# Thirty-two modulation rows of a fused transformer kernel moved from GpSimd to VectorE chains beside the first expert tables

## The reference, cut to what matters

```python
for l in range(DEPTH):                      # first block, DEPTH = 2
    mod = silu(c) @ mod_w[l] + mod_b[l]
    sh1, sc1, g1, sh2, sc2, g2 = split(mod, 6)
    h = rmsnorm(x) * (1 + sc1) + sh1
    y = gla_mixer(h) if l == 0 else swa_sink_attention(h, k_sh, v_sh)
    x = x + g1 * y
    h = rmsnorm(x) * (1 + sc2) + sh2
    x = x + g2 * peer(h)                    # u = u_tab[e], gelu(h . u), times gate, times v_tab[e]
    # behind layer 0: shared keys and values, with a modulation of their own
# second block: one layer, retention + latent attention with (sh1, sc1, g1), experts with (sh2, sc2, g2)
```

## Time and profile before

| | |
|---|---|
| median of 3 runs | 3168.49 us (3166.95 to 3172.3) |
| the profiled execution: its own time | 3162.82 us |
| its span | 3161.0 us |
| mean granted clock of TensorE | 0.972 |
| PE / DVE / ACT / POOL busy | 2972.8 / 2045.1 / 1586.9 / 1596.7 us |
| bytes read from memory | 550.17 MB |

### The profile page before, as it was taken

One profiled execution on the slowest core, in us unless ns is written; L12 is line 12 of the kernel. 1 busy time (PEld: TensorE's weight loads), 2 busy tenths in 40 slices (PEclk: granted clock), 3 DMA queues, 4 the chain that ended last, 5 costly groups with the idle time before them and its releaser, 6 DMA issues.

```text
span 3161.0 us, 57822 instructions
## 1 busy us (share of the span) xinstructions
PE 2972.8 (94%) x18908; PEld 2689.0 (85%) x18908; DVE 2045.1 (65%) x3383; ACT 1586.9 (50%) x3103; POOL 1596.7 (51%) x1261
## 2 busy tenths in 40 slices
PE   7989999988999986999999799999899999999998
PEld 6779999987787875899999677887789789999997
DVE  6648960058888878389200888887883446777776
ACT  1124555577555543355555965554454224555554
POOL 5868898986544445159989844443470010000100
PEclk8989999999999997999999999999999999999998
DMA  7545555522766632345555056664464235555553
GB/s 249 206 155 182 184 180 182 183 73 94 258 233 228 230 137 87 128 155 185 179 181 190 7 186 244 231 234 175 176 224 134 93 127 193 192 192 195 192 192 125
DMA packets 153462, 552.56 MB, mean 175 GB/s; under 512 B 16896, under 2 KB 19712, under 8 KB 153232
## 3 DMA queue, kind: packets, MB, share of 16 engines
q1 hardware_dynamic: 151136, 547.42, 49.9%
q10 hardware_dynamic: 2224, 3.87, 0.4%
HBM read 550.17 MB, written 1.05 MB: 174 GB/s over the span
## 4 chain that ended last, share of the span: by engine, by line
PE 75%; ACT 7%; DVE 6%; issue 5%; POOL 5%; DMA 1%; ACTq 0%; DVEq 0%; SPq 0%; POOLq 0%
PE bank L953 23%; PE bank L979 21%; PE bank L1224 12%; PE bank L1245 6%; PE bank L749 5%; ACT hT L1453 3%; PE bank L697 3%; POOL arena L2562 2%; POOL arena L2564 1%; ACT hT L1449 1%; DVE w_parts L1775 1%; POOL arena L2566 1%; DMA arena<-stream 1%; ACT h_parts L1461 1%; POOL arena L2574 1%
## 5 line engine op out<-in xcount | busy, mean ns | idle before, releaser
L2514 POOL TENSOR_TENSOR w_parts<-ring,w_parts 128x512 fp32r<-128x512 f32 x512 | 665.4, 1308 | 160.6 <-ACT w_parts L1413 113.2
L953 PE MATMUL bank<-h_parts,w_parts 128*128 128x256 f32 x6144 | 738.2, 284 | 3.9 <-POOL w_parts L2514 3.9
L953 PEld LDWEIGHTS bank<-h_parts,w_parts 128*128 128x128 f32 x6144 | 737.5, 192 | 4.3 <-POOL w_parts L2514 4.3
L2562 POOL TENSOR_TENSOR arena<-arena,cact 128x1024 f32<-128x1024 f32 x80 | 165.6, 2070 | 733.5 <-DMA arena<-stream 733.4
L1413 ACT ACTIVATE w_parts<-ring 128x512 fp32r<-128x512 f32 x512 | 323.1, 632 | 319.8 <-PE bank L953 307.6
L1224 PEld LDWEIGHTS bank<-h_parts,w_parts 128*128 128x128 f32 x3072 | 374.8, 193 | 3.9 <-DVE arena L2376 1.5
L1224 PE MATMUL bank<-h_parts,w_parts 128*128 128x256 f32 x3072 | 375.8, 284 | 1.4 <-DVE arena L2376 1.4
L1611 ACT ACTIVATE w_parts<-ring 128x512 fp32r<-128x512 f32 x384 | 242.3, 632 | 266.3 <-PE bank L1224 172.2
L979 PE MATMUL bank<-w_parts,a_parts 128*128 128x512 f32 x1536 | 370.2, 397 | 1.6 <-DVE a_parts L2156 1.6
L979 PE MATMUL bank<-h_parts,a_parts 128*128 128x512 f32 x1536 | 364.5, 393 | 5.6 <-DVE a_parts L2156 5.5
L2445 DVE TENSOR_TENSOR w_parts<-ring,w_parts 128x512 fp32r<-128x512 f32 x376 | 272.4, 736 | 147.7 <-ACT w_parts L1611 144.6
(11 more groups left out here) (339 smaller groups left out, 4628.8 us busy)
## 6 DMA issues: line engine op xcount, KB each, us to landing
ring<-stream SPq DMA_DIRECT2D x786, 512.0 KB, 3.3
arena<-stream SPq DMA_DIRECT2D x192, 512.0 KB, 4.3
hT<-stream SPq DMA_DIRECT2D x32, 512.0 KB, 4.7
mean<-stream SPq DMA_DIRECT2D x32, 512.0 KB, 4.6
arena<-consts ACTq DMA_DIRECT2D x1, 1536.0 KB, 6.6
xT<-xin ACTq DMA_DIRECT2D x1, 1024.0 KB, 10.7
out<-hT SPq DMA_DIRECT2D x4, 256.0 KB, 2.2
arena<-subk ACTq DMA_DIRECT2D x2, 128.0 KB, 2.2
```

The costliest lines, as they stand in the source:

```text
L953: mm = pe.matmul(bank[k][:, 0:T], w[:, wp, ws], h_parts[:, hp, 4 * j + q, :], start=(j == 0 and q == 0 and i == 0), stop=(j == 1 and q == ...
L2514: pool.tensor_tensor(w[:, 1, :], ring[(base + k) % RING][:, j * 512:(j + 1) * 512], w[:, 0, :].bitcast(F32), ALU.subtract).then_inc(sem(f" ...
L2562: pool.tensor_tensor(b3, b3, c_b, ALU.mult).then_inc(sem("mod_step"), 1)
```

## The change

Rows 88 to 103 are now made beside the last 32 tiles of the first table of layer 0, rows 136 to 151 beside those of layer 1 (`UP_FROM` = 96, `UP_ROWS` = 16). SP loads each row into one half of `hT` (two buffers), in `up_loads`, two rows for every four tiles. DVE makes a row in eight dependent steps of 128 x 128 (`up_mods_dve`): one scaled copy from SBUF to PSUM, six times "chunk times scalar plus sum" in PSUM bank 6, and a last one whose output goes to a part in `rs`. The two rows of a turn alternate. PE does the column product behind every second tile, into bank 7, and at the end DVE adds the bias to 16 columns at once. From the attention stage and the mixer the row loads, the POOL work, the column products and the bias additions are gone.

```diff
-MODS_SWA = (88, 104)
-MODS_MIX = (136, 152)
+MODS_UP = ((88, 104), (136, 152))
+UP_ROWS = 16
+UP_FROM = NK - 2 * UP_ROWS
...
+        def up_buffer(i):
+            return hT[:, 4 * i:4 * i + 4, :].rearrange("p c t -> p (c t)")
+        def up_part(i):
+            return rs[:, i * P:(i + 1) * P]
+        def up_loads(sp, l):
+            u, row = MO[f"peer{l}_u"][0], mod_row(MODS_UP[l][0])
+            at = u + UP_FROM
+            def slots(it, lo, hi):
+                for k in range(lo, hi):
+                    s = (at + k) % RING
+                    sp.wait_ge(ring_free, it * RING + (at + k + 1))
+                    sp.dma_start(ring[s][:, :], stream[it * RING + (main_row(at) + k)]).then_inc(landed[s], 16)
+            for i in range(2):
+                sp.wait_ge(ring_free, at)
+                sp.dma_start(up_buffer(i), stream[row + 3 * i]).then_inc(up_landed[i], 16)
+            with sp.Fori(0, UP_ROWS // 2 - 1) as it:
+                for i in range(2):
+                    slots(it, 2 * i, 2 * i + 2)
+                    sp.wait_ge(sem("up_made"), it * 2 + (UP_ROWS * l + i + 1))
+                    sp.dma_start(up_buffer(i), stream[it * 6 + (row + 3 * (i + 2))]).then_inc(up_landed[i], 16)
+            slots(UP_ROWS // 2 - 1, 0, RING)
...
-            loads(MO["peer0_u"][0], after_v[0])
+            loads(MO["peer0_u"][0], MO["peer0_u"][0] + UP_FROM)
+            up_loads(sp, 0)
...
-            loads_with_mods(kv, MO["peer1_q"][0], MODS_SWA, MODS_SWA[0], at)
-            loads(MO["peer1_q"][0], after_v[1])
+            loads(kv, MO["peer1_q"][0])
+            loads(MO["peer1_q"][0], MO["peer1_u"][0] + UP_FROM)
+            up_loads(sp, 1)
...
-            loads_with_mods(mix, MO["mix_out"][1], MODS_MIX, MODS_MIX[0], [mix + 5 * i // 2 for i in range(16)])
+            loads(mix, MO["mix_out"][1])
...
-            up_pe(pe, l, ROUTE_TILE, NK)
+            up_pe(pe, l, ROUTE_TILE, UP_FROM)
+            if l == 0:
+                pe.sem_inc(sem("up_column"), 2)
+            up_pe(pe, l, UP_FROM, NK, rows=True)
...
+                    if rows and k % 2:
+                        i = k // 2
+                        pe.wait_ge(sem("up_made"), it * 2 + (UP_ROWS * l + i + 1))
+                        column(pe, bank[7][:, bass.ds(it * 2 + i, 1)], up_part(i)).then_inc(sem("up_column"), 1)
...
-            project_norm(pe, "swa_out", A.o, "w_out", "1b", between={5: lambda: [mods_pe(pe, MODS_SWA, g) for g in (11, 12)]})
+            project_norm(pe, "swa_out", A.o, "w_out", "1b")
...
-            mods_pe(pe, MODS_MIX, 17)
...
-            mods_pe(pe, MODS_MIX, 18)
...
+        def up_mods_dve(dve, l):
+            lo, hi = MODS_UP[l]
+            sums = [bank[6][:, i * P:(i + 1) * P] for i in range(2)]
+            c = cact[:, 8 * l:8 * l + 8]
+            steps = 2 * (DC - 1)
+            with dve.Fori(0, UP_ROWS // 2) as it:
+                for k in range(DC):
+                    for i in range(2):
+                        w = up_buffer(i)[:, k * P:(k + 1) * P]
+                        if k == 0:
+                            dve.wait_ge(up_landed[i], it * 16 + 16 * (UP_ROWS // 2 * l + 1))
+                            dve.tensor_scalar(sums[i], w, c[:, 0:1], None, ALU.mult).then_inc(sem("up_step"), 1)
+                            continue
+                        dve.wait_ge(sem("up_step"), it * steps + (UP_ROWS // 2 * steps * l + 2 * k - 1 + i))
+                        if k < DC - 1:
+                            dve.scalar_tensor_tensor(sums[i], w, c[:, k:k + 1], sums[i], ALU.mult, ALU.add)\
+                               .then_inc(sem("up_step"), 1)
+                        else:
+                            dve.wait_ge(sem("up_column"), it * 2 + (UP_ROWS * l + i + 1))
+                            dve.scalar_tensor_tensor(up_part(i), w, c[:, k:k + 1], sums[i], ALU.mult, ALU.add)\
+                               .then_inc(sem("up_made"), 1)
+            dve.wait_ge(sem("up_column"), UP_ROWS * (l + 1) + 2)
+            dve.tensor_tensor(modv[:, lo:hi], bank[7][:, 0:hi - lo], V("mod_b")[:, lo:hi], ALU.add).then_inc(signal("dve_step"), 1)
+            dve.wait_ge(sem("dve_step"), signalled("dve_step"))
...
             dve.tensor_scalar(mean[:, 3, :], route[:, 2, :], -1.0, None, ALU.mult).then_inc(sem(f"{n}_negated"), 1)
+            up_mods_dve(dve, l)
             dve.wait_ge(sem(f"{n}_gelu"), NK)
...
-            for g in (11, 12):
-                mods_dve(dve, g)
...
-            behind[("mla_cq", 2)] = lambda: mods_dve(dve, 17)
...
-            mods_dve(dve, 18)
...
-            mods_pool(pool, MODS_SWA, 0)
             peer_pool(pool, 1)
-            mods_pool(pool, MODS_MIX, 1)
```

More of the change, by code:

```diff
@@ L300, in block_program @@
         ring_free = sem("ring_free")
+        up_landed = [sem(f"up_landed{i}") for i in range(2)]
         full = [sem(f"bank_full{i}") for i in range(4)]
@@ L473, in mod_row, with main_row @@
             return SO[f"peer{l}_v"][0] + 3 * (m - (40, 104)[l]) + 2
+        def main_row(i):
+            return i + (40 - FIRST_MODS if i >= FIRST_MODS else 0) + sum(V_ROWS for at in after_v if i >= at)
         def mod_buffers(seg):
@@ L509, in mod_number @@
         def mod_number(m):
-            return m - FIRST_MODS
+            return m - FIRST_MODS - sum(hi - lo for lo, hi in MODS_UP if m >= hi)
+        def up_buffer(i):
[19 more added lines that the diff above has]
+            slots(UP_ROWS // 2 - 1, 0, RING)
         @block.sync
         def _(sp):
-            def main_row(i):
-                return i + (40 - FIRST_MODS if i >= FIRST_MODS else 0) + sum(V_ROWS for at in after_v if i >= at)
             def load(i):
@@ L781, in mods_pe @@
             parts = mod_parts(seg)
[L782 removed]
+            pe.wait_ge(sem("mod_made"), mod_number(8 * g + 7) + 1)
             t = open_tile(f"mods{g}")
@@ L938, in peer_pe, with up_pe @@
             back_pe(pe, n, "kv" if l == 0 else "mid", {0: ((act_y, 1), (dve_y, 1)), 2: ((act_y, 2), (dve_y, 2))})
-        def up_pe(pe, l, first, last):
+        def up_pe(pe, l, first, last, rows=False):
             n = f"p{l}"
-            with pe.Fori(first // 4, last // 4) as it:
+            with pe.Fori(0, (last - first) // 4) as it:
                 for k in range(4):
@@ L946, in up_pe @@
                         half = 2 * k + j
-                        pe.wait_ge(sem(f"{n}_low"), it * 8 + (half + 1))
+                        pe.wait_ge(sem(f"{n}_low"), it * 8 + (2 * first + half + 1))
                         w = w_parts[half % HALVES]
```

12 lines of the change are left out of this document (removed).

## The result

The changed kernel takes **3140.74 us** (median of four runs, 3138.13 to 3149.34), the kernel before beside it 3169.19: ratio 0.9914, interval 0.9893 to 0.9935, so 28.5 us shorter. Its profiled execution took 3140.26 us, with a span of 3137.8, 23.2 less than the span before. Forecast were 3136 us and 32.4 us gained.

The account below looks back on a forecast made before the run. PE was taken as the bound, the attention stage as bound by handoffs, with POOL and DVE slowing each other. Gains of 41.4 us less 7.0 and 2 gave 32.4, so 3136 us; own range 3128 to 3152, 8 in 10 3125 to 3155.

Parts of the forecast that it names:

- Rival B: Beside the first table, DVE's steps in PSUM wait for POOL: about 3273 us, slower than before; chance 0.05.
- C: Attention stage and mixer bound by something other than POOL, most waits stay: a gain of 20 us, 3148; chance 0.12.
- D: Whole kernel: no change, within 0.2%, as A and C together; chance 0.05.
- rival A: Beside the first table, the ring starves a little behind SP's waits: 20 us lost instead of 2, 3154; chance 0.10.
- Attention, split projections: Six split projections in the attention stage: PE's waits and slow matmuls go, 12 us gained, bounds 6 and 13.2.
- Rotations: Eight rotations of the queries in the attention stage, at 1.52 us each undisturbed: 7.9 us gained, bounds 6 and 8.
- Mixer's projections: Split projections and token form in the mixer: PE's waits for DVE's low parts go, 12 us gained, bounds 6 and 13.3.
- Column groups: Groups of column products leave the output projection, 5.6 us gained, and the mixer, 3.9 us gained.
- New column products: 32 column products on PE beside the first tables, 0.22 us each: 7.0 us lost, bounds 4.5 and 9.
- DVE's chain: DVE's row steps beside the first table: 0.34 us each, 5.4 us per turn of 11.5, hidden because DVE is idle.
- The loads beside it: Row loads among the first table's ring tiles: hidden with 1 us to spare, 2 us lost for both layers.

## Why the prediction was right, and where not

The time lies 4.7 us above the forecast and inside its own range (whose low end comes to 3129 by its own terms, not 3128). The main mechanism held: the waits of the two stages went with the rows, and DVE's new steps were hidden. Rivals B, C and D did not come about; A did in kind, at less than half of its price. That the time came so near is partly luck, as the steps show:

**Attention, split projections** (12 us, bounds 6 and 13.2): mis-sized. From 1154.32 to 1205.97 PE needs 51.7 us, where it was 67.0 from 1143.22 to 1210.19: 15.3 us, above the upper bound. The window of the earlier trace rows left out two waits at the small rotation products (1.2 us), and the 1.2 us set aside for handoffs that would remain were not needed. **Rotations** (7.9): 9.0 us, 20.0 to 11.0 (1206.60 to 1217.62), at 1.38 each; the 1.52 taken for an undisturbed one had POOL beside it too (L2566 and L2574, 1214.24 to 1215.68), and its last step took 0.56 us where it is 0.42 now. **Mixer's projections** (12): over the whole mixer PE's two groups of split projections, with their waits, fell from 166.7 to 152.3 us, so 14.4; without POOL's arithmetic alone the rest became 15.4 shorter. Both are over the bound of 13.3, which came from the window of the earlier trace rows alone. Waits of 2.7 us remain in the mixer. **Column groups** (5.6 + 3.9): 5.3 + 2.8 measured, the second within the scatter of its stage. Sum forecast 41.4, in the trace 49.8.

**New column products** (7.0): (375.5 - 372.2) / 16 = 0.21 each, 6.6 us in all.

**DVE's chain** (0.34 us a step, hidden): 0.348, and hidden. The first step of a row was left between 0.295 and 1.21 us; it takes 0.354 into PSUM with POOL at work. The trace agrees with the Trainium skill (VectorE: DVE Perf Modes, section "What auto-detection actually checks"), by which such a copy takes the mode with both ports only where source and destination lie in SBUF. Rival B had decided from 0.47 us a step. A row's last step, whose output goes to SBUF, takes 0.344 us too: L1888 of the earlier trace rows, the slow one of the same kind, has a second input from SBUF, which none of these has.

**The loads beside it** (2 us for both layers): mis-sized most, at 6.0 us in this trace and 9.9 in the kernel's second one. Without a stall a first table takes 375.5 us at a clock of 1.00 and 377.0 at 0.86. So it cost 379.4 - 377.0 = 2.4 us in layer 0 and 380.6 - 377.0 = 3.6 in layer 1, of which 1.5 is the lower clock behind the stall; then 6.1 and 3.8. The ring tile landed in 4.1 us at the median in layer 0, under the 4.4 taken, and yet the cover of 1 us was not there. Two things were wrong. The first turn was dismissed as jitter, but it sends two row loads out together, and that is where layer 1 stalled. And in layer 0 later turns idled too, up to 5.1 us in six waits. The prediction had named this as a sign of being wrong (ACT's waits for the ring over 2 us, with PE idle behind POOL's low parts), and it came: 30.9 us, and 2.0 in each layer. It is rival A's mechanism, not its size: a DMA share of 0.68 came, not the 0.81 of rival A, and 6 to 10 us, not 20.

**Not in the sum at all**: how each stage finds the clock, 3.0 us in the two first tables, and 10.1 us in the second ones. Too small gains (8.4 short) and costs left out (4.0 of loads, 3.0 and 10.1) cancelled in part, and that is luck. The sum of 32.4 us was made for the pair of traces, and these show 23.2, 9.2 less; the medians show 28.5.

## What to carry to other kernels

Work moved onto an idle engine is paid elsewhere: here by the products on the engine that has no slack, by the transfers, and perhaps by the stage behind. Spread such transfers over as many steps as there are: one row in three tiles instead of two took 7.5 us off the two first tables. Where they can't be spread, start the first ones early and apart. When a wait is added, look for what stands behind it on that queue, counts for other engines above all. And a change of 0.2% (6 us) can't be read from one trace: two traces of the same kernel had spans 6.7 us apart, and one untouched stage 3.5. Compare the stages, with the clock of their first microseconds.

## What the runs showed of the hardware

PE was busy for all of the first 12 us of the second tables, and still got through 31, 39 or 46 matmuls of the same code, by the granted clock (0.57, 0.72, 0.86); in two kernels traced twice seven of eight stage starts found the same clock. Behind 2.00 us without work in the first table the next 48 matmuls took 7.49 us instead of 6.00. DVE instructions with both inputs in SBUF, 0.42 us each without POOL, took 1.77 and 1.37 beside POOL's wide ones and ended 0.29 us behind them; without POOL's arithmetic DVE's low part in the mixer fell from 1.079 to 0.702 us. And DVE's scalar-tensor steps with their running sum in PSUM start every 0.27 us or less beside a busy POOL, where the same kind of instruction from SBUF to SBUF took 1.13.
